# Half of the second modulation pieces and the first gate, summed by GpSimd products and ScalarE row sums in the second head-pair group

## The reference, cut to what matters

```
mod = silu(c) @ w_ada + b_ada                        # c: one row of 1024; w_ada: 1024 x 6144
sh1, sc1, gt1, sh2, sc2, gt2 = split(mod, 6)
h   = layer_norm(x) * (1 + sc1) + sh1
p   = h @ w_in                                       # gMLP half and RWKV-7 half, 12 pieces of columns
mix = concat(y_a, y_b) @ w_out                       # y_a: spatial gating, y_b: the recurrent half
x1  = layer_norm(ALPHA * x + gt1 * mix) * ln1_g + ln1_b
h   = x1 * (1 + sc2) + sh2                           # "second modulation": sh2, sc2
f   = (silu(h @ Wg) * (h @ Wu)) @ w_ffn_out
x2  = layer_norm(ALPHA * x1 + gt2 * f)               # then the second block
```

## Time and profile before

| what | value |
|---|---|
| times of three runs | 1408.68, 1412.06, 1412.5 us; median 1412.06 |
| the profiled execution | 1413.13 us, span 1411.3 us (1.83 us lie around the span) |
| PE busy | 1337.2 us (95%) |
| DVE, ACT, POOL busy | 760.9 (54%), 569.0 (40%), 435.0 us (31%) |
| mean granted TensorE clock | 0.979 of full speed |
| DMA | 147.92 MB, mean 105 GB/s |
| chain that ended last, by engine | PE 76%, DVE 15%, DMA 3%, ACT 3%, issue 2%, POOL 2% |

### The profile page before, as it was taken

The page is one execution under the profiler, slowest core; times in us unless marked ns, Lnnn a source line. Parts: engine busy times, 40 slices in busy tenths (PEclk is TensorE's granted clock), DMA queues, the critical chain, the costliest instruction groups (busy, mean ns, idle before and its releaser), DMA issues.

```text
span 1411.3 us, 22545 instructions
## 1 busy us (share of the span) xinstructions
PE 1337.2 (95%) x9338; PEld 1110.5 (79%) x9338; DVE 760.9 (54%) x1246; ACT 569.0 (40%) x855; POOL 435.0 (31%) x123
## 2 busy tenths in 40 slices
PE   3999898898999999999999999999999999999998
PEld 2778786787788888888888787777798888888886
DVE  7778688764665444344327538787265444453002
ACT  4344466253442222321126545655364334433212
POOL 0143233023314433345422320000213433443344
PEclk7899899999999999999999999999999999999999
DMA  7755400302222333223322610101312232223211
GB/s 268 298 220 209 149 3 3 104 22 90 90 90 104 136 134 135 90 90 119 104 78 91 243 61 31 61 31 60 105 60 90 90 113 96 90 90 125 99 60 60
DMA packets 24747, 147.92 MB, mean 105 GB/s; under 512 B 2720, under 2 KB 3872, under 8 KB 9032
## 3 DMA queue, kind: packets, MB, share of 16 engines
q1 hardware_dynamic: 21120, 134.21, 26.8%
q10 hardware_dynamic: 3528, 12.28, 2.4%
HBM read 144.36 MB, written 4.74 MB: 106 GB/s over the span
## 4 chain that ended last, share of the span: by engine, by line
PE 76%; DVE 15%; DMA 3%; ACT 3%; issue 2%; POOL 2%; SPq 0%; DVEq 0%; ACTq 0%; POOLq 0%
PE bank L2165 22%; PE bank L2167 21%; PE bank L2166 21%; PE bank L2433 4%; DVE raw L1785 3%; DMA raw<-in_weights 2%; PE bank L1198 1%; ACT weight_hi L1386 1%; POOL weight_lo L1336 1%; PE bank L1191 1%; DVE xres L1736 1%; PE bank L1182 1%; DVE act_lo L1733 1%; POOL xres L1367 1%; DVE bank L1729 1%
## 5 line engine op out<-in xcount | busy, mean ns | idle before, releaser
L1336 POOL TENSOR_TENSOR weight_lo<-raw,weight_hi 128x2048 fp32r<-128x2048 f32 (+2 forms) x84 | 388.1, 4620 | 859.1 <-ACT weight_hi L1386 859.1
L2165 PE MATMUL bank<-act_hi,weight_hi 128*128 128x512 f32 (+1 forms) x1136 | 436.5, 384 | 18.2 <-DVE act_lo L1733 12.2
L2167 PE MATMUL bank<-act_hi,weight_lo 128*128 128x512 f32 (+1 forms) x1136 | 425.7, 375 | 0.0
L2166 PE MATMUL bank<-act_lo,weight_hi 128*128 128x512 f32 (+1 forms) x1136 | 425.5, 375 | 0.0
L1386 ACT ACTIVATE weight_hi<-raw 128x2048 fp32r<-128x2048 f32 (+1 forms) x98 | 185.3, 1891 | 430.8 <-PE bank L2167 395.6
L2165 PEld LDWEIGHTS bank<-act_hi,weight_hi 128*128 128x128 f32 x1136 | 215.5, 190 | 67.4 <-issue 17.8
L2167 PEld LDWEIGHTS bank<-act_hi,weight_lo 128*128 128x128 f32 x1136 | 215.4, 190 | 39.2
L2166 PEld LDWEIGHTS bank<-act_lo,weight_hi 128*128 128x128 f32 x1136 | 215.9, 190 | 35.1 <-issue 0.2
L2166 PE MATMUL bank<-weight_lo,hid_hi 128*128 128x512 f32 x352 | 136.9, 389 | 0.0
L2165 PE MATMUL bank<-weight_hi,hid_hi 128*128 128x512 f32 x352 | 136.9, 389 | 0.0
L2167 PE MATMUL bank<-weight_hi,hid_lo 128*128 128x512 f32 x352 | 136.9, 389 | 0.0
(11 more groups left out here) (375 smaller groups left out, 1796.4 us busy)
## 6 DMA issues: line engine op xcount, KB each, us to landing
raw<-in_weights SPq DMA_DIRECT2D x120, 1024.0 KB, 4.8
w<-in_w ACTq DMA_DIRECT2D x2, 2048.0 KB, 11.9
bias_rows<-bias_rows_once ACTq DMA_DIRECT2D x1, 2560.0 KB
xres<-in_x SPq DMA_DIRECT2D x4, 512.0 KB, 6.6
strip<-bias_rows ACTq DMA_DIRECT2D x1, 2048.0 KB, 8.2
out<-xres SPq DMA_DIRECT2D x3, 512.0 KB, 2.6
row_a<-in_ln_g ACTq DMA_DIRECT2D x2, 512.0 KB, 4.1
row_b<-in_ln_b ACTq DMA_DIRECT2D x2, 512.0 KB, 5.4
```

Source lines behind the costliest of these rows:

```text
L1336: pool.tensor_tensor(wlo[i % SPLIT][:, :size], raw[n % RAW][:, :size], whi[i % SPLIT][:, :size], ALU.subtract).then_inc(lo_ready, 1)
L2165: pe.matmul(o, l[0], r[0], start=first, stop=False)
L2166: pe.matmul(o, l[0], r[1], start=False, stop=False)
L2167: return pe.matmul(o, l[1], r[0], start=False, stop=last)
```

## The change

Only the first four `ada1` pieces stay in the first stage. The other four, and the four `ada2` pieces, are called `LATE_ADA` and stand in the stream behind pu1, eight units of 1 MB, ahead of `w_out`. Their sums are taken in the second head-pair group, by two engines: GpSimd multiplies a piece in place by `c_row` (`ada_rows`: two products of 128 x 1024), ScalarE sums each row of the product (`ada_sums`: two activations with an accumulated output), and after g2 VectorE adds the biases and makes the columns for all of them in six small instructions (`late_columns`). A buffer of `raw` is free for SP when ScalarE has summed both halves (`ada_summed`).

```diff
-ADA_BEHIND = {"r0": 1, "r1": 1, "v0": 2, "v1": 1, "pv0": 2, "pv1": 1}
-ADA_BESIDE = {"k1": 1, "r0": 2, "r1": 1, "v0": 2, "v1": 1, "pv0": 1}
+ADA_BEHIND = {"r0": 1, "r1": 1, "v0": 1, "v1": 1}
+ADA_BESIDE = {"k1": 1, "r0": 1, "r1": 1, "v0": 1}
+EARLY_ADA = sum(ADA_BEHIND.values())
+LATE_ADA = [f"ada1_{k}" for k in range(EARLY_ADA, 8)] + [f"ada2_{n}" for n in range(4)]
...
-    units += gates[0]
+    units += second + gates[0]
...
-    1: {("ta", 1): [("ada", 0)], ("mv", 0): [("prep", 2, 13), ("ada", 1)], ("mv", 1): [("ada", 2)], ("q2", 1): [("ada", 3)],
-        ("q4", 0): [("prep", 3, 13)]}}
+    1: {("n", 1): [("ada_rows", 0)], ("mv", 0): [("prep", 2, 13)], ("q2", 0): [("ada_rows", 1)], ("q2", 1): [("ada_sums", 0), ("ada_rows", 2)],
+        ("q4", 0): [("prep", 3, 13)], ("q4", 1): [("ada_sums", 1), ("ada_rows", 3)], ("tb", 0): [("ada_sums", 2), ("ada_rows", 4)],
+        ("tb", 1): [("ada_sums", 3), ("ada_rows", 5)], ("r3", 1): [("ada_sums", 4), ("ada_rows", 6)], ("m", 1): [("ada_sums", 5), ("ada_rows", 7)],
+        ("m2", 1): [("ada_sums", 6)], ("z4", 1): [("ada_sums", 7)], ("g2", 1): [("ada_columns",)]}}
...
# SP
-                    sp.wait_ge(ada_used, m + 1 - sum(1 for i in SPLIT_UNITS if i < m))
+                    if UNITS[m][0] in LATE_ADA:
+                        sp.wait_ge(S["ada_summed"], 2 * LATE_ADA.index(UNITS[m][0]) + 2)
+                    else:
+                        sp.wait_ge(ada_used, sum(1 for u in UNITS[:m + 1] if u[1] == "w_ada" and u[0] not in LATE_ADA))
...
# GpSimd
+            elif kind == "ada_rows":
+                n = UNIT_AT[LATE_ADA[args[0]]]
+                raw_ready(pool, n)
+                for j in range(2):
+                    w = raw[n % RAW][:, DM * j:DM * j + DM]
+                    o.done(pool.tensor_tensor(w, w, c_row, ALU.mult), S["ada_rows"])
...
# ScalarE
+            elif kind == "ada_sums":
+                i, name = args[0], LATE_ADA[args[0]]
+                for j in range(2):
+                    w = raw[UNIT_AT[name] % RAW][:, DM * j:DM * j + DM]
+                    k = EARLY_ADA + i
+                    total = ...
+                    act.wait_ge(S["ada_rows"], 2 * i + j + 1)
+                    a.done(act.activation(w, w, ACT.Copy, accum_out=total), S["ada_summed"])
...
# VectorE
+        def late_columns():
+            ...
+            dve.wait_ge(S["ada_summed"], 2 * len(LATE_ADA))
+            tt(gate_cols[:, 0, :], gate_cols[:, 0, :], pc[:, COLS["b_gt1"]:COLS["b_gt1"] + KC], ALU.add, sem=S["gate_sums"])
+            tt(scale, scale, modc[:, ks], ALU.add)
+            tt(affine[:, 2, ks], scale, part("ln1_g"), ALU.mult)
+            tt(affine[:, 3, ks], affine[:, 3, ks], part("b_sh2"), ALU.add)
+            tt(scale, scale, part("ln1_b"), ALU.mult)
+            tt(affine[:, 3, ks], affine[:, 3, ks], scale, ALU.add, sem=S["affine1"])
...
-            elif kind == "ada":
-                gate_sums(0, *args)
+            elif kind == "ada_columns":
+                late_columns()
```

More of the change, by code:

```diff
@@ L629, in build @@
                                           "out", "rel", "tabs", "w1", "once", "strip0", "strip", "rows3", "rows4")}
-    S = {n: sem(n) for n in ("summed", "gated", "row2_ready", "eps_ready", "silu_c", "column_ready", "gate_sums", "future_ready", "xn_ready", "affine1", "shift_ready", "lora_ready",
+    S = {n: sem(n) for n in ("summed", "gated", "row2_ready", "eps_ready", "silu_c", "column_ready", "gate_sums", "ada_rows", "ada_summed", "future_ready", "xn_ready", "affine1", "shift_ready", "lora_ready",
                              "kk_raw", "kk_sq", "cs_ready", "exp_ready", "minus_ready", "r_ready", "ep_ready", "rows_free", "root_ready", "inverse_ready", "norm_root", "prep_ready",
@@ L1603, in _ @@
                 chunk_act(*args)
+            elif kind == "ada_sums":
[3 more added lines that the diff above has]
+                    k = EARLY_ADA + i
+                    total = gate_cols[:, 0, 2 * i - KC + j:2 * i - KC + j + 1] if name[3] == "2" else (affine[:, 3, k:k + 1], modc[:, KC + k:KC + k + 1])[j]
+                    act.wait_ge(S["ada_rows"], 2 * i + j + 1)
+                    a.done(act.activation(w, w, ACT.Copy, accum_out=total), S["ada_summed"])
             elif kind == "first_hi":
@@ L1804, in second_column, with gate_sums @@
             ts(affine[:, 2, k:k + 1], scale, col("ln1_g", k))
[L1805 to L1811, removed]
+            stt(affine[:, 3, k:k + 1], scale, col("ln1_b", k), affine[:, 3, k:k + 1], ALU.mult, ALU.add)
+        def late_columns():
+            ks = slice(EARLY_ADA, KC)
+            part = lambda name: pc[:, COLS[name] + EARLY_ADA:COLS[name] + KC]
+            scale = modc[:, KC + EARLY_ADA:2 * KC]
+            dve.wait_ge(S["ada_summed"], 2 * len(LATE_ADA))
[5 more added lines that the diff above has]
+            tt(affine[:, 3, ks], affine[:, 3, ks], scale, ALU.add, sem=S["affine1"])
+        def gate_sums(n):
+            ada_sums(f"ada3_{n}", [col("b_gt2", 2 * n + j) for j in range(2)], [gate_cols[:, 1, 2 * n + j:2 * n + j + 1] for j in range(2)])
             d.step(V.tensor_copy(stats[:, 0, 0:1], stats[:, 0, 0:1]), S["gate_sums"])
@@ L1875, in bonus_dve @@
             tt(rT[:, p, :], bank(("bonus", p))[:], vT[:, p, :], ALU.mult, sem=drain(("bonus", p), "dve"))
-        seconds = iter(range(KC))
+        seconds = iter(range(EARLY_ADA))
         for n, name in enumerate(W_IN1):
@@ L2118, in _ @@
             if m in GATE_AT:
-                gate_sums(1, GATE_AT.index(m))
+                gate_sums(GATE_AT.index(m))
             if m == FT - 3:
@@ L2650, in _ @@
             if m == GATE_ROWS_AT:
-                pe.wait_ge(S["gate_sums"], KC)
+                pe.wait_ge(S["gate_sums"], 1 + KC // 2)
                 for j in range(2):
```

2 lines of the change are left out of this document (1 added, 1 removed).

## The result

| kernel | median of the runs | profiled execution |
|---|---|---|
| before | 1411.15 us (9 runs, 1408.68 to 1413.52) | 1413.13 us, span 1411.3, clock 0.979 |
| changed | 1414.51 us (9 runs, 1411.34 to 1417.50) | 1414.9 us, span 1413.1, clock 0.984 |

The ratio is 1.0024, with an interval from 1.0015 to 1.0033: 3.4 us slower (2.1 to 4.7), which is clear of no change, but less than the 0.3% that the prediction calls no change. The forecast was +4.1 us. The two profiled executions differ by 1.8 us only, so they make the change look 1.6 us better than the medians do.

The account below looks back on a forecast made before the run. In the second group it took TensorE as the bound, with ScalarE, which empties PSUM between stages, short of time. The terms -9.1 + 7.1 + 3.1 + 3.0 gave +4.1 us, hence 1416.2 us, range 1407 to 1423.

Parts of the forecast that it names:

- first stage: From 154 us: pu0 waits for the fourth piece, not the seventh, so TensorE's hole goes; gain 9.1 us, bounds 5.5 to 9.4.
- ScalarE's sums: Second group, 290 to 310 us: 14.73 + 12.4 = 27.1 us of ScalarE work in 20 us, so 7.1 us late.
- GpSimd stops VectorE: Norm steps beside r2 to m2: VectorE waits for GpSimd's products through a shared port lock; 3.1 us, bounds 0 and 6.
- columns and the collision at `act_lo`: Between g2 and the state chain: six instructions wait for GpSimd's low part, then VectorE's `act_lo` for GpSimd's; 3.0 us, bounds 0.3 and 3.3.
- the lower end of 5.9: Second group: lower end of the 7.1 us ScalarE loss, since ScalarE also sat idle for 1.21 us just ahead, at 289.80.
- one of the six column instructions lasting 3 us or more: Sign in the changed trace, between g2 and the state chain: a VectorE column instruction lasts 3 us or more.
- The ring costs nothing: Second group: GpSimd's products stay ahead of ScalarE's sums by 3 us or more, so three buffers cost nothing; 5 us otherwise.
- By the same amount to the end: Sign: from the `w_out` stage on, everything is later than before by 4 us, by the same amount to the end.
- the ring: Rival, second group: the buffers pace ScalarE, which stands waiting in front of its sums; up to 5 us more, 1421; chance 0.15.
- TensorE hides the sums: Rival, second group: copies have slack, the loss stays near 4 us with no lock; -5.1 us, 1407; chance 0.13.
- ScalarE's load alone: Rival, second group: the lock costs little and the columns fit into idle time, 1.0 us; sum -1.0, 1411; chance 0.24.
- It doesn't do what it says: Rival, first stage: pu0 stays late, held by the fourth piece's sum; gain only 3 us, sum +10.2, 1422; chance 0.05.

Follow-up runs that it names:

- narrow_both: Changed kernel with GpSimd's products and ScalarE's row sums both cut to 8 elements of a row instead of 1024: 1405.48 us, ratio 0.9943.
- late1: Kernel before with the changed stream, but VectorE sums the eight late pieces, seven in the second group and one in the w_out stage: 1402.70 us, ratio 0.9936.
- stream_only: Kernel before with ada1_4 to ada1_7 moved behind pu1 in the stream, VectorE still summing all eight in the first stage: 1411.63 us, ratio 1.0001.
- sums_behind_z4: Changed kernel with the seventh pair of row sums moved from ahead of ScalarE's z4(2) copies to behind those of z4(3): 1413.38 us, ratio 1.0004.
- The narrow kernels: Changed kernel cut to 8 elements a row in GpSimd's products (1411.35 us), ScalarE's sums (1409.49 us) or both (1405.48 us).
- transfers_later: Kernel before with the second and third w_out units transferred only once m2(2)'s f result has left PSUM: 1412.43 us, ratio 1.0008.

## Why the prediction was right, step by step

| term | predicted | measured |
|---|---|---|
| first stage | -9.1 (5.5 to 9.4) | -9.7 at its end (one clock); of that -8.0 is left at the end with both narrow, -9.0 with late1 |
| ScalarE's sums | +7.1 | +7.2 |
| GpSimd stops VectorE | +3.1 (0 to 6) | +4.9 |
| columns and the collision at `act_lo` | +3.0 (0.3 to 3.3) | 0 |
| sum | +4.1 | +3.4 |

The measured rows add up to +4.1, since the two loads together cost 0.7 us less than one by one; each row is uncertain by 2 to 2.5 us.

**First stage: right, in mechanism and nearly in size.** The hole, ScalarE's `sq` and the half clock went, as said, and stream_only shows that pu0's place in the stream does it. The chunk stage began at 174.95 us (177 predicted). The gain of 9.7 us at one clock is a little above the upper bound of 9.4. The pair of traces shows about 1.5 us more, since the kernel before also ran at 0.97 of the clock between 105 and 154 us and the changed one at 1.00, 1.5 us over 48.88 us. That is not the change's: narrow_both, with the same stream, ran at 0.97 from 106 to 145.

**ScalarE: right in size, and partly by luck.** A pair costs 2.1 us and not 2.48. With that, the rule I used (busy work above the window's length) gives 14.73 + 10.5 - 20 = 5.2 us and not 7.1, and 7.2 were measured, within 2.5. Its premise, that ScalarE never waits, didn't hold either: it waited 2.18 us for a stopped norm step at 284.68. The rule doesn't know where a pair stands, and the seventh alone, in front of z4's copies, makes a wait of 2.3 us, which sums_behind_z4 shows. (The 1.21 us behind the lower end of 5.9 stand in the trace, but not in the earlier trace rows, which the prediction names.)

**The lock: right in kind, too small.** I let one of each pair be stopped for half a product, 0.9 us. Five of eight were, for 1.45 to 2.10 us each, since each started early in a product. Of these 9 us about half reached TensorE (4.9, within 2.5).

**The columns: wrong.** The failed step is "then `act_lo` wants the same lock at 318.6 while GpSimd's own `act_lo` runs". The stop on the first instruction came as predicted, 2.25 us:

```profile
314.41 2.25 DVE L1754 TENSOR_TENSOR gate_columns<-gate_columns,params 128x8 f32<-128x8 f32 x1
...
317.68 0.48 DVE L2017 SCALAR_TENSOR_TENSOR hs<-bank,chunk_decay,hs 128x64 f32<-128x64 f32 x2
320.40 1.23 DVE L1754 TENSOR_TENSOR act_lo<-uT,act_hi 128x1024 fp32r<-128x1024 f32 x1 [2.24 <-ACT act_hi L1605]
```

But `act_lo` waits for ScalarE's `act_hi`, and that for y(2), which had moved with TensorE; VectorE was again idle for 2.24 us and then started 1 us ahead of GpSimd (321.39). I had left `act_hi` at its old time while I moved everything before it. The chain that ended last, asked for 275 to 325 us, passes the six instructions by:

```profile
314.64 0.48 PE bank L2617 x4
315.12 3.68 PE bank L2465 x64
318.83 0.60 ACT y L1545
319.43 0.95 ACT act_hi L1605
320.40 1.24 DVE act_lo L1754
```

`act_lo` is late because TensorE is: after its holes it runs at 0.66 of the clock from 310 to 330 us (0.83 before), and yl(2)'s 64 products in this chain took 3.7 us at half clock, where they took 2.5 at the full clock before. Of the signs that the prediction named, "one of the six column instructions lasting 3 us or more" thus failed, with 2.25 us.

**Not in the sum:** the w_out units' transfers now come late, and the "issue" hole at the start of g2 grew from 0.4 to 2.0 us; and the lower clock that follows TensorE's holes, 3.4 us of the 12.6 that the second group lost. The narrow kernels don't part its price from that of the waits ahead of it. "The ring costs nothing" held for the sums, and missed what its late turns do behind them. "By the same amount to the end" holds from 335 us on, with 1.4 to 1.8 us in this pair of traces and not 4.

The rivals: the ring fell, since no sum waited. "TensorE hides the sums" fell with 7.2 us. "ScalarE's load alone" was right on the columns and wrong on the lock: 4.9 us, not 1.0. "It doesn't do what it says" fell with the hole at 154 us. That the sum was close is luck in part: the columns' 3 us, which weren't there, stood in for a lock that was 2 us larger and for the gain that was lost again behind the first stage (9.7 us at its end, 8.0 at the kernel's), which I had at nothing.

## What to carry over

Work that is moved to an idle engine is paid at two places that a busy share doesn't show: in its queue, ahead of a copy that a stage waits for, and on the engine that it shuts out. Look first for idle time of the engine that already does it in one instruction: 2.6 us of VectorE a piece became 4.7 of GpSimd and 2.1 of ScalarE. When an instruction is delayed in an estimate, move all that follows from it, the other engine's part of a collision too.

## What was not expected of the hardware

- VectorE instructions of 1 to 8 elements a row are shut out as long as large ones: tensor_scalar on 128x8, 0.17 us alone, took 1.80 and 2.12 us beside GpSimd, and tensor_tensor on 128x8 2.25. In late1 a scalar_tensor_tensor on 128x1 (0.22 us alone) took 4.17 us and ended with GpSimd's low part.
- Where weight transfers that no one waits for came late, TensorE's "issue" hole between small products was wider: 1.20 us (transfers_later) and 2.03 (changed) against 0.38. In transfers_later the hole lay behind the transfers and not beside them; why is open.
- Kernels with the same first stage show either 0.96 to 0.97 or 1.00 of TensorE's clock between 106 and 146 us, with TensorE full in both. A pair of single profiles is thus uncertain by 1.5 us there, nearly half of what was measured.
